# The down layer of a squared-ReLU MLP as seven block products for each chunk of 1024 features instead of eight, on one Trainium2 core

## The reference

```python
def squared_relu_mlp(h, w_up, w_down):
    u = jax.nn.relu(h @ w_up)
    return (u * u) @ w_down
...
        x = x + (merged.astype(dt) @ w_o[l]).astype(dt)
        h2 = _rms(x, norm2_g[l]).astype(dt)
        x = x + squared_relu_mlp(h2, w_up[l], w_down[l]).astype(dt)
    return x[:, BLOCK:]
```

## Time and profile before

| | us |
|---|---|
| median of 3 runs | 1192.71 (1192.49 to 1193.37) |
| the profiled execution, its own time | 1193.66 |
| its span, first to last instruction | 1191.9 |
| PE busy in the span | 1174.0 |
| DVE busy | 499.2 |
| ACT busy | 491.0 |
| POOL busy | 468.1 |

### The profile page before, as it was taken

How to read it: one execution, slowest core, us unless ns; L and a number is a source line. 1 busy time by engine, 2 the same in 40 slices (tenths; PEclk the granted TensorE clock), 3 DMA queues, 4 the chain that set the end, 5 groups by cost and what they waited for, 6 DMA issues and landing times.

```text
span 1191.9 us, 20669 instructions
## 1 busy us (share of the span) xinstructions
PE 1174.0 (98%) x8782; PEld 963.1 (81%) x8782; DVE 499.2 (42%) x994; ACT 491.0 (41%) x808; POOL 468.1 (39%) x288
## 2 busy tenths in 40 slices
PE   8999999999999999999999999999999999999998
PEld 7998877887798688667777777778888888888887
DVE  4699425454554643442452675262522000222000
ACT  6455423323323534765726544433634221343220
POOL 3443435335343234333323622343444544344541
PEclk9999999999999999999999999999999999999999
DMA  6222323122222152212522312342223332222330
GB/s 252 89 71 89 108 90 108 57 86 97 90 73 73 36 164 67 65 36 73 193 75 67 106 53 64 107 148 71 88 89 102 111 106 89 78 99 94 118 124 36
DMA packets 35998, 111.47 MB, mean 94 GB/s; under 512 B 4273, under 2 KB 9137, under 8 KB 35394
## 3 DMA queue, kind: packets, MB, share of 16 engines
q1 hardware_dynamic: 30288, 98.59, 24.9%
q10 hardware_dynamic: 5106, 11.43, 2.7%
q0 software_dynamic: 512, 0.13, 0.1%
HBM read 99.43 MB, written 9.04 MB: 91 GB/s over the span
## 4 chain that ended last, share of the span: by engine, by line
PE 83%; DVE 8%; ACT 4%; POOL 2%; issue 2%; DMA 0%; DVEq 0%; ACTq 0%
PE pst L1856 19%; PE pst L1858 18%; PE pst L1857 17%; PE pst L2032 5%; PE pst L2031 5%; PE pst L2030 5%; POOL w_lo L818 1%; PE pst L2371 1%; ACT w_hi L936 1%; PE pst L2363 1%; PE pst L2096 1%; PE pst L2149 1%; PE pst L2348 1%; PE pst L2333 1%; DVE cdif L1418 1%
## 5 line engine op out<-in xcount | busy, mean ns | idle before, releaser
L818 POOL TENSOR_TENSOR w_lo<-raw,w_hi 128x1024 fp32r<-128x1024 f32 x164 | 401.9, 2455 | 632.4 <-ACT w_hi L936 620.7
L1856 PE MATMUL pst<-h_hi,w_hi 128*128 128x512 f32 (+1 forms) x704 | 257.1, 365 | 1.3 <-DVE h_lo L1391 0.7
L1858 PE MATMUL pst<-h_hi,w_lo 128*128 128x512 f32 (+1 forms) x704 | 243.3, 346 | 0.0
L1857 PE MATMUL pst<-h_lo,w_hi 128*128 128x512 f32 (+1 forms) x704 | 242.9, 345 | 0.0
L936 ACT ACTIVATE w_hi<-raw 128x1024 fp32r<-128x1024 f32 x164 | 172.1, 1054 | 140.2 <-PE pst L2032 114.1
L1856 PEld LDWEIGHTS pst<-h_hi,w_hi 128*128 128x128 f32 x704 | 133.4, 189 | 25.9 <-issue 5.4
L1857 PEld LDWEIGHTS pst<-h_lo,w_hi 128*128 128x128 f32 x704 | 133.6, 190 | 15.7 <-issue 2.9
L1858 PEld LDWEIGHTS pst<-h_hi,w_lo 128*128 128x128 f32 x704 | 133.3, 189 | 15.9
L1856 PE MATMUL pst<-x_hi,w_hi 128*128 128x512 f32 (+1 forms) x272 | 102.6, 377 | 0.4 <-DVE x_lo L1722 0.4
L1857 PE MATMUL pst<-x_lo,w_hi 128*128 128x512 f32 (+1 forms) x272 | 102.4, 377 | 0.0
L1858 PE MATMUL pst<-x_hi,w_lo 128*128 128x512 f32 (+1 forms) x272 | 102.4, 376 | 0.0
(11 more groups left out here) (339 smaller groups left out, 1991.8 us busy)
## 6 DMA issues: line engine op xcount, KB each, us to landing
raw<-in_weights SPq DMA_DIRECT2D x164, 512.0 KB, 3.3
xt<-in_x SPq DMA_DIRECT2D x4, 512.0 KB, 5.4
wait_gate<-stage ACTq DMA_DIRECT2D x8, 256.0 KB, 2.0
gate_t<-wait_gate ACTq DMA_DIRECT2D x1, 2048.0 KB, 8.8
x<-in_x ACTq DMA_DIRECT2D x1, 2048.0 KB, 7.5
out<-x SPq DMA_DIRECT2D x7, 256.0 KB, 3.9
cst<-in_consts SPq DMA_DIRECT2D x1, 1524.0 KB, 11.3
wait_ret_g<-stage ACTq DMA_DIRECT2D x4, 256.0 KB, 2.2
```

The lines of the kernel that those rows point to most:

```text
L818: nc.gpsimd.tensor_tensor(w_lo[:, u % W_SLOTS, :], raw[:, u % RAW_SLOTS, :], w_hi[:, u % W_SLOTS, :].bitcast(F32), ALU.subtract).then_inc( ...
L1856: M(out, lh, rh, start=(first and i == 0), stop=False)
L1857: M(out, lh, rl, start=False, stop=False)
L1858: last = M(out, ll, rh, start=False, stop=(final and i == len(terms) - 1))
```

## The change

The MLP is now done in four chunks of 1024 features: 8 `up` jobs and then 14 `down` jobs, four times. For the down layer of a chunk, the tokens, the features and the output columns are each cut in two, which gives a 2 x 2 by 2 x 2 block product with blocks of 256 tokens by 512 features and 512 features by 512 columns. It is computed with seven block products (`PRODUCTS`) in a variant of Strassen's scheme. A product m has two jobs (j = 0, 1), each with one weight unit of its own and 12 matmuls of 512 moving columns.

- Three products (m = 0, 1, 6) use a block of the weights as it is. In the other four, the weights are a difference, which DVE makes in `raw` in place (`weight_sums`), each from its own block and the block or difference of an earlier product (`LESS`). ACT then makes the high part as before. The low part of these units is made by DVE (`weight_lows`), that of all others by POOL.
- A block of the weights is loaded anew for each product that needs it: 56 `down` units instead of 32. Three more `raw` slots are used from the MLP's first unit on, so that unit u waits for unit u-6. SP also waits until the last difference that reads a slot has been made.
- On the activations' side, ACT takes the ReLU to `usq`, DVE multiplies it with the ReLU of the PSUM bank (which now empties the bank), and ACT copies the high parts. For each pair of `up` jobs, DVE makes four sums or differences (`usum`), ACT their high parts (`u_sum_hi`) and DVE their low parts (`u_sum_lo`).
- Each product has two PSUM banks out of three pairs. DVE reads them out after each product: it adds them to the blocks of `x2` that they belong to (`GOES_TO`). Products 0 and 3, which belong to four and three blocks, are gathered over the first three chunks in `shared`; in the last chunk they are added straight to the blocks, and the gathered sums are spread over `x2` by `share_out` in the `up` jobs 1 and 3 of that chunk.

Cut to its core, the diff is:

```diff
-FH = DFF // P // 2
+FC = 8
+NFC = DFF // P // FC
+UP_ORDER = [0, 4, 1, 5, 2, 6, 3, 7]
...
+U11, U12, U22, S1, S2, S3, S4 = range(7)
+PRODUCTS = [("p11", U11, (0, 0)), ("p12", U12, (1, 0)), ("p51", S1, (0, 1)), ("p62", S2, (1, 1)),
+            ("p42", U22, (1, 0)), ("p73", S3, (0, 0)), ("p34", S4, (1, 1))]
+LESS = {2: 0, 3: 2, 4: 3, 5: 3}
+GOES_TO = [None, [(0, 0)], [(0, 1), (1, 1)], None, [(1, 0)], [(1, 0), (1, 1)], [(0, 1)]]
+NM = len(PRODUCTS)
+SHARED = {0: [(0, 0), (0, 1), (1, 0), (1, 1)], 3: [(0, 1), (1, 0), (1, 1)]}
...
+def down_jobs(c):
+    return [("down", c, (m, j)) for m in range(NM) for j in range(2)]
+
+
+JOBS = (PHASE_C + PHASE_A + PHASE_B + PHASE_D + PHASE_E + proj_jobs(BRANCH_SW) + PHASE_O +
+        [j for c in range(NFC) for j in up_jobs(c) + down_jobs(c)])
...
+RAW_MORE = 3
+LESS_UNIT = {UNIT_NO[("w_down", c, (m, j))]: UNIT_NO[("w_down", c, (LESS[m], j))]
+             for c in range(NFC) for m in LESS for j in range(2)}
...
+        def low_done(u):
+            if u in LESS_UNIT:
+                return lo_summed, 2 * NB + SUM_NO[u] + 1
+            return lo_ready, u + 1 - sum(v < u for v in LESS_UNIT)
...
+        def down_bank(g, t):
+            return [(4, 5), (6, 7), (1, 3)][g % 3][t]
...
+                held = u - RAW_SLOTS if u < FFN0 + RAW_MORE else u - RAW_SLOTS - RAW_MORE
+                sp.wait_ge(*low_done(held))
+                if held in LAST_SUM:
+                    sp.wait_ge(raw_summed, KD + LAST_SUM[held] + 1)
...
+                    if u in LESS_UNIT:
+                        continue
 
                     pool.wait_ge(hi_ready, u + 1)
-                    nc.gpsimd.tensor_tensor(w_lo[:, u % W_SLOTS, :], raw[:, u % RAW_SLOTS, :],
+                    nc.gpsimd.tensor_tensor(w_lo[:, u % W_SLOTS, :], raw_unit(u),
...
+                    act.wait_ge(*raw_loaded(u))
+                    if u in LESS_UNIT:
+                        act.wait_ge(*sums_done(u))
...
+                    i, p, q = kind_no(n), b // 2, usq[:, b // 2 % 2, b % 2, :]
+                    act.wait_ge(dense_done, n + 1)
+                    if i >= 4:
+                        act.wait_ge(u_lo_ready, 3 * (i // 2 - 1))
+                    A(q, one, ACT.Relu).then_inc(u_hi_ready, 1)
                     act.wait_ge(job_out[kind], i + 1)
-                    if a == 1 and b == 0:
-                        act.wait_ge(dense_done, n)
-                    A(u_hi[:, b, :], ub[:, i % 2, :], ACT.Square).then_inc(u_hi_ready, 1)
+                    if b % 2 == 0:
+                        A(u_hi[:, p, U11, :], q[:, 0:TH], ACT.Copy).then_inc(u_hi_ready, 1)
+                    else:
+                        A(u_hi[:, p, U12:U22 + 1, :], halves(q), ACT.Copy).then_inc(u_hi_ready, 1)
+                        act.wait_ge(usum_ready, KD + i // 2 + 1)
+                        A(s_hi_[:, p], usum[:, p % 2], ACT.Copy).then_inc(u_hi_ready, 1)
...
+                    i, p, par_ = kind_no(n), b // 2, b // 2 % 2
+                    weight_sums(UNIT_NO[units_of(JOBS[n])[0]] + RAW_SLOTS + RAW_MORE)
+                    weight_lows(converted_after(n - 1))
+                    q = usq[:, par_, b % 2, :]
+                    dve.wait_ge(u_hi_ready, 5 * (i // 2) + 2 * (b % 2) + 1)
+                    V.scalar_tensor_tensor(out=q, in0=one, scalar=0.0, in1=q, op0=ALU.max, op1=ALU.mult)\
+                        .then_inc(job_out[kind], 1)
+                    if b % 2 == 0:
+                        dve.wait_ge(job_out[kind], i + 1)
+                        dve.wait_ge(u_hi_ready, 5 * (i // 2) + 2)
+                        V.tensor_tensor(u_lo[:, p, U11, :], q[:, 0:TH], u_hi[:, p, U11, :].bitcast(F32), ALU.subtract)\
+                            .then_inc(u_lo_ready, 1)
+                    else:
+                        dve.wait_ge(job_out[kind], i + 1)
+                        u11, u21, u12, u22 = (usq[:, par_, k // 2, TH * (k % 2):TH * (k % 2) + TH] for k in range(4))
+                        sums = usum[:, par_]
+                        link(V.tensor_tensor(sums[:, 0], u21, u22, ALU.add))
+                        link(V.tensor_tensor(sums[:, 1], sums[:, 0], u11, ALU.subtract))
+                        V.tensor_tensor(sums[:, 2], u21, u11, ALU.subtract)
+                        V.tensor_tensor(sums[:, 3], u12, sums[:, 1], ALU.subtract).then_inc(usum_ready, 1)
+                        dve.wait_ge(u_hi_ready, 5 * (i // 2) + 4)
+                        V.tensor_tensor(u_lo[:, p, U12:U22 + 1, :], halves(q), u_hi[:, p, U12:U22 + 1, :].bitcast(F32),
+                                        ALU.subtract).then_inc(u_lo_ready, 1)
+                        dve.wait_ge(u_hi_ready, 5 * (i // 2) + 5)
+                        V.tensor_tensor(s_lo_[:, p], sums, s_hi_[:, p].bitcast(F32), ALU.subtract).then_inc(u_lo_ready, 1)
+                    if a == NFC - 1 and b in (1, 3):
+                        share_out(b // 2)
...
+                    m, j = b
+                    weight_sums(UNIT_NO[units_of(JOBS[n])[0]] + RAW_SLOTS + RAW_MORE)
+                    weight_lows(converted_after(n))
+                    if j == 0:
+                        return
+                    g = NM * a + m
+                    if g:
+                        dve.wait_ge(job_out["down"], g)
...
+                    for t in range(2):
+                        o = pst[:, down_bank(g, t), :]
+                        if m in SHARED and a < NFC - 1:
+                            e = shared[:, min(m, 1), t, :]
+                            last = V.tensor_tensor(e, o, e, ALU.add) if a else V.tensor_copy(e, o)
+                        else:
+                            for rq in GOES_TO[m] or SHARED[m]:
+                                last = V.tensor_tensor(x2_part(rq, t), o, x2_part(rq, t), ALU.add)
+                    last.then_inc(job_out["down"], 1)
+
+            summed, lowered = [0], [FFN0]
+
+            def weight_lows(upto_unit):
+                for v in range(lowered[0], min(upto_unit, NU)):
+                    if v in LESS_UNIT:
+                        dve.wait_ge(hi_ready, v + 1)
+                        V.tensor_tensor(w_lo[:, v % W_SLOTS, :], raw_unit(v), w_hi[:, v % W_SLOTS, :].bitcast(F32),
+                                        ALU.subtract).then_inc(lo_summed, 1)
+                lowered[0] = max(lowered[0], upto_unit)
+
+            def weight_sums(upto_unit):
+                for v in range(max(summed[0], FFN0), min(upto_unit, NU)):
+                    if v in LESS_UNIT:
+                        less = LESS_UNIT[v]
+                        dve.wait_ge(*raw_loaded(v))
+                        dve.wait_ge(*(sums_done(less) if less in LESS_UNIT else raw_loaded(less)))
+                        V.tensor_tensor(raw_unit(v), raw_unit(v), raw_unit(less), ALU.subtract).then_inc(raw_summed, 1)
+                summed[0] = max(summed[0], upto_unit)
+
+            def share_out(t):
+
+                if t == 0:
+                    dve.wait_ge(job_out["down"], NM * (NFC - 1))
+                e1, e6 = shared[:, 0, t, :], shared[:, 1, t, :]
+                V.tensor_tensor(x2_part((0, 0), t), e1, x2_part((0, 0), t), ALU.add)
+                link(V.tensor_tensor(e6, e6, e1, ALU.add))
+                for rq in SHARED[3]:
+                    last = V.tensor_tensor(x2_part(rq, t), e6, x2_part(rq, t), ALU.add)
+                link(last)
...
+                    g, which = NM * a + m, PRODUCTS[m][1]
+                    if j == 0 and g >= 3:
+                        pe.wait_ge(job_out["down"], g - 2)
+                    pe.wait_ge(*low_done(u))
                     us = u % W_SLOTS
-                    for j in range(2):
-                        f = 2 * kk + j
-                        ws = slice(T * j, T * j + T)
-                        for blk in range(NB):
-                            if c == 0 and f == 0 and blk >= 2:
-                                pe.wait_ge(job_out["up"], FH * (a + 1) + blk - NB + 1)
-                            o = pst[:, down_bank(c, blk), :]
-                            toks = slice(P * blk, P * blk + P)
-                            M(o, u_hi[:, f, toks], w_hi[:, us, ws], start=(f == 0), stop=False)
-                            M(o, u_hi[:, f, toks], w_lo[:, us, ws], start=False, stop=False)
-                            last = M(o, u_lo[:, f, toks], w_hi[:, us, ws], start=False, stop=(f == FH - 1))
-                            if n == len(JOBS) - 1 and j == 1 and blk < NB - 1:
-                                last.then_inc(rows_done, 1)
+                    ends = n == len(JOBS) - 1
+                    for kk, t in ([(0, 0), (1, 0), (0, 1), (1, 1)] if ends else [(0, 0), (0, 1), (1, 0), (1, 1)]):
+                        p, ws = 2 * j + kk, slice(T * kk, T * kk + T)
+                        if t == 0:
+                            pe.wait_ge(u_lo_ready, operand_split(a, which, p))
+                        last = product3(pst[:, down_bank(g, t), :],
```

(80 more changed lines are left out.)

86 lines of the change are left out of this document (34 added, 52 removed).

## The result

The changed kernel takes 1203.15 us, median of 4 runs (1202.90 to 1203.34), beside 1192.80 (1192.49 to 1193.37) for the kernel before: 1.0086 times as long, 95% interval 1.0069 to 1.0104. The prediction said 1203.3.

The account below looks back on a forecast made before the run. PE alone was taken to bound the MLP. Waits of 15.9 us in the first three chunks and 16.4 in the last, minus 21.8 for removed matmuls, gave about +10.6 and 1203.3 us; forecast range 1198 to 1209.

Parts of the forecast that it names:

- What PE gives up: Down stages: 672 matmuls instead of 768, 96 fewer at 0.2267 us, taking 21.8 us off PE.
- Exclusion of DVE and POOL: DVE instructions with two SBUF inputs and POOL's low parts wait for each other; +10.6 us with it, -9.7 without.
- The third unit: At d2, a chunk's third down unit, PE waits 2.4 us for the high part behind ACT's work, then POOL's low part.
- DVE's queue: Down stage: DVE's differences, low parts and adds run late, making PE's delay 5.3 us at d9 in each ordinary chunk.
- the dearer DVE: Rival: DVE's 1024-column instructions cost their whole 1.22 us, giving 1211.5 us, up to 1219 with repeated contention; chance 0.20.
- The banks: Down stage: a product's adds come within the two products (10.9 us) PE has in hand, so they cost nothing.
- The last chunk: The fourth chunk loses more than the others: 5.3 + 3.4 + 1.8 + 3.6 + 2.3 = 16.4 us.
- (a): Last chunk's up jobs: `share_out`'s adds delay DVE, so PE waits 0.5 and 2.6 us, with restarts 3.4.
- (b): Last chunk: d4's difference falls behind POOL's low part of d1, making d2 1.8 us later.
- (c): Last chunk: product 0 has 8 adds instead of 2, costing 3.6 us, which reach d5 in full.
- (d): Last chunk: product 3's 6 adds instead of 2 put d11's low part behind POOL's of d13; 2.3 us with restart.
- The clock: Rival: after PE's waits one product of 24 matmuls runs at 1.2 GHz, costing 5.4 us more, 1209 us; chance 0.06.

Follow-up runs that it names:

- e6: The changed kernel with six slots instead of four for `w_hi` and `w_lo` from the first down unit on, and one more of `raw`; 1183.53 us.
- e9: e6 with the two `share_out` calls moved from up jobs 1 and 3 of the last chunk to jobs 0 and 2; 1178.45 us.
- e4: The changed kernel with one operand of DVE's differences (except d4's) and low parts read from PSUM, so it computes something else; 1193.82 us.
- e7: e6 with products 0 and 3 gathered in `shared` in the last chunk too, and `share_out` in its down jobs; 1180.87 us.
- e2: The changed kernel with ACT making the next weight unit's high part before that of the sums in odd up jobs; 1201.70 us.

## Why the prediction was right, step by step

- **What PE gives up.** 21.8 us from 96 matmuls at 0.2267. Shown by e6 and e9, whose chunks take 81.60 us.
- **Exclusion of DVE and POOL.** As read from the earlier trace rows. e4 takes it away in the down part and is 9.3 us faster.
- **The third unit.** Predicted 2.4, measured 2.41 to 2.46, in every chunk.
- **DVE's queue.** Predicted 5.3 a chunk, measured 5.1 to 5.2, with waits at the units named. The distance of 1.13 for 1024 columns was the middle of three values and is the one that the trace shows; the dearer DVE did not come.
- **The banks.** Predicted to cost nothing, and PE waits at none of d4, d6, d8, d10 and d12, before which it could wait for a bank. This holds for the kernel after; in e9 they are what is left of the loss.
- **The last chunk.** Predicted 16.4, measured 16.6, in part by errors that cancel. (a) Waits with restarts of 3.8 instead of 3.4. (b) did not come: d2 waited 2.45, not 4.2; the 1.8 us of that step are wrong. DVE's difference of d4 was meant to fall behind POOL's low part of d1; it began at 1146.58, POOL's low part at 1146.62, so that POOL waited instead (3.43 us), and d2 came no later than in the other chunks. (c) and (d) are there: the down part lost 16.6 - 3.8 - 1.7 = 11.1, where the prediction without (b) has 11.2. (d) has the form that was predicted: DVE's low part of d11 takes 3.10 us (from 1186.77) behind POOL's, which starts at 1186.42. The wait at d5 is 2.64 instead of 3.7, and the 0.6 at d3 is missing, since that time was lost before, at half clock: 2.45 + 1.6 + 2.64 is 6.7, as are the predicted 2.4 + 0.6 + 3.7.
- **The clock.** It got a chance of 0.06, and it did fall, four times. It cost little: in the first and third chunk, and behind d2 of the last, PE had to wait for DVE later in any case. Only the fall at 1137.7, in an up job, cost its 1.7 us, about what (b) was too much. That these two cancel is luck, and with it that the total came within 0.2 us. The page "TensorE: Matmul & The Clock Gate" of the Trainium skill (HAM oscillation) warns of such falls after idle gaps. This trace has them, but behind shorter gaps than that section has in mind (2.41 to 2.77 us), and here the measurement decides. The price that I had given for one fall (a whole product, 5.4 us) was three times too high.
- **What I did not ask** is why DVE began so late. The prediction took the lead of the queues as given, and charged DVE's load against PE's time from d0 on. That gives the right time for this kernel, but it points at making DVE's work less or cheaper, and the larger gain lay elsewhere. e4, which takes the exclusion off DVE's 1024-column instructions and computes something else, gained 9.3 us; e6, with all the work left in, gained 19.6, and in it the second and third chunk lose nothing.

Two things stay open. In the first chunk of e6, e7 and e9 PE waits 1.1 us at d4, for DVE's low part, and 0.8 at d10, for the adds of product 2; why only there was not tried. The added slots begin with that chunk's down units, which may be it. And why the clock fell behind some waits of 2.4 to 2.8 us and not behind others is not settled.

## What to carry to other kernels

When a job gets shorter, count how far ahead its helpers may work in time, not in slots: four slots were 21.8 us of PE's work before and 10.9 after, and two more slots for the parts, with one more for the weights, turned +0.9% into -0.8% (with `share_out` moved, -1.2%). When that wait is gone, look for the next resource with few places: here the PSUM banks (e9). Removing one wait in front of a late queue moves the wait, it doesn't remove it (e2); find the last unit at which PE waits, and count what the queue has to do up to there. Work put off to the end can leave PE's path and come back on the output's: against e6, e7's last chunk lost 7.0 us less and its tail was 3.8 longer.
